# One decoder step on one core: the first projection chunk before the normalisation is known, its weights loaded ahead of the small vectors

## What is computed

```python
def _rmsnorm(x, g):
    y = xf * lax.rsqrt(jnp.mean(xf * xf, axis=-1, keepdims=True) + EPS)
    return (y * g.astype(jnp.float32)).astype(x.dtype)

# _mixer(h = _rmsnorm(x, norm_mix_g), ...)
proj = h @ w_in                                   # 1024 -> 7168 columns
cv, cg, q, f, v, og, ga, gb = jnp.split(proj, _split_offsets(), axis=-1)
u = cv * jax.nn.sigmoid(cg)
full = jnp.concatenate([conv_state.astype(u.dtype), u], axis=1)
c = lax.conv_general_dilated(full, conv_dw_w[:, None, :], ...)   # 31 taps, depthwise
...
# then the HGRN2 branch, gates, w_out, residual; norm; mixture of 32 experts; residual; norm
```

## Time and profile before

| | |
|---|---|
| median of three runs | 830.75 us (830.71 to 831.6) |
| the profiled execution | 830.96 us, its span 828.4 us |
| TensorE busy | 786.7 us, 95% of the span |
| TensorE weight loads | 453.0 us, 55% |
| VectorE busy | 246.6 us, 30% |
| ScalarE busy | 154.1 us, 19% |
| GpSimd busy | 120.8 us, 15% |
| moved by DMA | 267.99 MB, 324 GB/s over the span |

### The profile page before, as it was taken

How to read it: one execution, slowest core, us unless ns; L and a number is a source line. 1 busy time by engine, 2 the same in 40 slices (tenths; PEclk the granted TensorE clock), 3 DMA queues, 4 the chain that set the end, 5 groups by cost and what they waited for, 6 DMA issues and landing times.

```text
span 828.4 us, 9578 instructions
## 1 busy us (share of the span) xinstructions
PE 786.7 (95%) x3929; PEld 453.0 (55%) x3929; DVE 246.6 (30%) x528; ACT 154.1 (19%) x242; POOL 120.8 (15%) x139
## 2 busy tenths in 40 slices
PE   6999999999999999999999999999989988999996
PEld 4888888888788888873333333333323222333332
DVE  2159958586552222361001110111011011101102
ACT  3012422434302500140111111100100110010012
POOL 5100051656520000001110000002200000000001
PEclk9999999999999999999999999999999999999999
DMA  8824656768589682389999999999999999999992
GB/s 302 255 102 148 232 158 204 194 188 192 191 285 408 247 302 102 115 306 416 422 398 429 426 427 426 426 425 428 426 429 425 428 427 429 427 423 421 423 419 109
DMA packets 74388, 267.99 MB, mean 324 GB/s; under 512 B 5598, under 2 KB 37450, under 8 KB 58335
## 3 DMA queue, kind: packets, MB, share of 16 engines
q1 hardware_dynamic: 72666, 264.36, 81.9%
q0 software_dynamic: 528, 1.90, 0.6%
q10 hardware_dynamic: 1149, 1.09, 0.4%
HBM read 259.26 MB, written 8.55 MB: 323 GB/s over the span
## 4 chain that ended last, share of the span: by engine, by line
PE 78%; DMA 13%; POOL 3%; DVE 2%; issue 2%; ACT 1%; SPq 1%; DVEq 0%; POOLq 0%
PE bank L1889 22%; PE bank L1529 21%; PE bank L1927 11%; DMA slots<-in_w_expert_gate_dram 8%; PE bank L1785 7%; PE bank L1936 6%; DMA slot<-in_w_expert_gate_dram 4%; PE bank L1732 2%; PE bank L1572 2%; DMA slots<-in_w_in_dram 1%; PE bank L1916 1%; DVE early L1396 1%; ACT wrep L953 1%; PE bank L1853 1%; PE bank L1800 1%
## 5 line engine op out<-in xcount | busy, mean ns | idle before, releaser
L1529 PE MATMUL bank<-hT,slots 128*128 128x264 f32 x896 | 207.2, 391 | 0.2 <-DMA slots<-in_w_in_dram 0.2
L1889 PE MATMUL bank<-slots,hT 128*64 128x512 f32 x680 | 185.6, 595 | 7.7 <-DMA slots<-in_w_expert_gate_dram 7.7
L1529 PEld LDWEIGHTS bank<-hT,slots 128*128 128x128 f32 x896 | 170.0, 192 | 28.9 <-issue 0.6
L1396 DVE TENSOR_TENSOR early<-early,bank 128x512 f32<-128x512 f32 x16 | 11.0, 688 | 384.6 <-PE bank L1889 384.6
L1889 PEld LDWEIGHTS bank<-slots,hT 128*64 128x64 f32 x680 | 57.1, 137 | 109.0 <-issue 96.9
L1927 PE MATMUL bank<-slots,wrep 128*64 128x512 f32 x336 | 103.6, 596 | 5.4 <-ACT wrep L953 5.4
L1889 PE MATMUL bank<-slot,hT 128*64 128x512 f32 x256 | 73.7, 594 | 2.3 <-DMA slot<-in_w_expert_gate_dram 2.3
L767 POOL COPY hT<-early 128x512 f32 x30 | 17.6, 613 | 369.6 <-PE bank L1889 286.3
L1936 PE MATMUL bank<-hT,diag 128*128 128x512 f32 x128 | 59.2, 605 | 0.2 <-ACT hT L965 0.2
L1927 PEld LDWEIGHTS bank<-slots,wrep 128*64 128x64 f32 x336 | 32.1, 137 | 49.7 <-issue 41.0
L1098 DVE SCALAR_TENSOR_TENSOR slot<-slot,rows_buf 128x256 f32<-128x256 f32 x120 | 48.1, 478 | 0.0
(11 more groups left out here) (292 smaller groups left out, 756.7 us busy)
## 6 DMA issues: line engine op xcount, KB each, us to landing
slots<-in_w_expert_gate_dram SPq DMA_DIRECT2D x18, 2048.0 KB, 28.3
slots<-in_w_expert_down_dram SPq DMA_DIRECT2D x18, 2048.0 KB, 29.6
slots<-in_w_expert_up_dram SPq DMA_DIRECT2D x16, 2048.0 KB, 29.9
slots<-in_w_in_dram SPq DMA_DIRECT2D x14, 2048.0 KB, 9.6
slot<-in_w_expert_gate_dram SPq DMA_DIRECT2D x8, 2048.0 KB, 25.3
slots<-in_w_expert_up_dram SPq DMA_DIRECT2D x9, 1024.0 KB, 29.8
slots<-in_w_expert_gate_dram SPq DMA_DIRECT2D x8, 1024.0 KB, 22.8
slot<-in_w_expert_up_dram SPq DMA_DIRECT2D x4, 2048.0 KB, 29.2
```

Source lines behind the costliest of these rows:

```text
L1396: dve.tensor_tensor(act.rearrange("s (f c) -> s f c", f=FT), act.rearrange("s (f c) -> s f c", f=FT), bank[UP][:, :].rearrange("s (c f) -> ...
L1529: last = mm(out, w[:, a, t * P:(t + 1) * P], hT[:, a, :], start=(a == 0), stop=(a == KT - 1))
L1889: last = mm(out[sl, :], xe[:, a, sl], expert_view(p, kind, e, a // 4)[:, a % 4, :], start=(a == 0), stop=(a == KT - 1))
```

## The change

Nothing of what is computed is left out. In `xgain` x times the norm weight is kept, and chunk 0 is projected from that; its four tiles are multiplied by the root when DVE takes them from PSUM. `hT`, for all other chunks, is `xgain` times the root.

- The norm weight for the mixer is loaded first of all, alone (`gain_in`), and its transposition is the first of the `misc` ring. Chunk 0 is loaded behind x in two halves (channel tiles 0 to 3 and 4 to 7), each with a semaphore of its own. The other eight vectors and the taps are issued from ACT's queue, behind ACT's copies to `xT`.
- x is turned to four banks of their own (4, 5, 2, 3), first all eight tiles of tokens 0 to 127, then those of 128 to 255; the samples are turned before both to bank 7. PE also makes six matmuls whose results nobody reads (`keep_busy`).
- PE begins chunk 0 with tiles 0 and 1 side by side over channel tiles 0 to 3 (`first_tiles(0)`), spreads the root, then channel tiles 4 to 7, then tiles 2 and 3. The vectors and the taps are turned behind chunk 0, and the products for the convolution state are moved behind chunk 1.

```diff
+            sp.dma_start(vecr[0:KT, :], ins["norm_mix_g"][0].rearrange("(r c) -> r c", c=P)).then_inc(gain_in, 16)
             sp.dma_start(xtok[0:NB, 2, :], xs).then_inc(x_in[2], 16)
             for i in range(2):
                 sp.dma_start(xtok[:, i, :], xp[i * P:(i + 1) * P, :]).then_inc(x_in[i], 16)
...
-            for c in range(STREAM):
+            sp.dma_start(slot3(0)[:, 0:KT // 2, :], stream[0][0][:, 0:KT // 2, :]).then_inc(first_in, 16)
+            sp.dma_start(slot3(0)[:, KT // 2:, :], stream[0][0][:, KT // 2:, :]).then_inc(stream_in[0], 16)
+            for c in range(1, STREAM):
                 load(c)
...
+            se.wait_ge(x_gained, 1)
+            se.copy(xT[:, :, SEQ:T], xs_turned).then_inc(x_copied, 1)
+            for i in range(KT // 2):
+                se.wait_ge(x_gained, 2 * i + 3)
+                se.copy(xT[:, 2 * i:2 * i + 2, 0:SEQ], x_pair(i)).then_inc(x_copied, 1)
...
+                se.dma_start(vecr[row:row + r, :], flat).then_inc(vec_in, 16)
+                row += r
+            assert row == 76
+            se.dma_start(tapr, ins["conv_dw_w"][0]).then_inc(tap_in, 16)
...
+            for d in range(KT):
+                dve.wait_ge(x_turned, d // 2 + 2)
+                dve.tensor_scalar(xgain[:, d, 0:SEQ], x_pair(d // 2)[:, d % 2, :], vec[:, d:d + 1], None,
+                                  ALU.mult).then_inc(x_gained, 1)
             dve.wait_ge(rms_ready, 1)
...
+            def normed(d):
+                dve.wait_ge(x_gained, KT + 1)
+                dve.tensor_tensor(hT[:, d, :], xgain[:, d, :], rstd, ALU.mult).then_inc(hmix_ready, 1)
...
+            def first_values(c):
+                src = take(proj, ("cv", c))
+                dve.tensor_tensor(u[:, c, :], src[:, 0:T], rstd, ALU.mult).then_inc(P_dve, 1)
...
+            pe.wait_ge(*made("ones"))
+            keep_busy(2)
+            pe.wait_ge(gain_in, 16)
+            misc.before_write(pe, "gain")
+            tr(bank[misc.bank("gain")][:, 0:KT], vecr[0:KT, :], ident[0:KT, 0:KT]).then_inc(M_ready, 1)
+            pe.wait_ge(x_in[2], 16)
+            for d in range(KT):
+                last = tr(xs_turned[:, d, :], xtok[0:NB, 2, d * P:(d + 1) * P], ident[0:NB, 0:NB])
+            last.then_inc(x_turned, 1)
+            keep_busy(4)
+            pe.wait_ge(x_in[0], 16)
+            for d in range(KT):
+                turn_x(d, 0)
...
+            first_tiles(0)
+            spread_rstd()
+            first_tiles(1)
+            for t in range(2, 4):
+                in_tile(0, t)
+            pe.wait_ge(vec_in, 16 * 8)
+            misc.before_write(pe, "vec")
+            tr(bank[misc.bank("vec")][:, 0:76], vecr, ident[0:76, 0:76]).then_inc(M_ready, 1)
             pe.wait_ge(tap_in, 16)
...
-            for t in range(1, 4):
-                in_tile(0, t)
+            in_projection(1)
```

More of the change, by code:

```diff
@@ L431, in _ @@
                 sp.dma_start(xtok[:, i, :], xp[i * P:(i + 1) * P, :]).then_inc(x_in[i], 16)
[L433 to L442, removed]
             def load(c):
@@ L815, in _ @@
                 se.activation(xjunk[0:m, i, :], xtok[0:m, i, :], ACT.Square, accum_out=ss[0:m, i:i + 1]).then_inc(x_squared, 1)
[L816 to L820, removed]
+            se.wait_ge(x_gained, 1)
[3 more added lines that the diff above has]
+                se.copy(xT[:, 2 * i:2 * i + 2, 0:SEQ], x_pair(i)).then_inc(x_copied, 1)
+            row = KT
+            for name, lead in (("b_gates", 0), ("conv_dw_b", 0), ("conv_ln_g", 0), ("conv_ln_b", 0),
+                               ("hgrn_lb_param", None), ("hgrn_norm_g", 0), ("norm_ffn_g", 0), ("norm_final_g", None)):
+                a = ins[name] if lead is None else ins[name][0]
+                flat = a.rearrange("l (r c) -> (l r) c", c=P) if name == "hgrn_lb_param" else a.rearrange("(r c) -> r c", c=P)
+                r = flat.shape[0]
+                se.dma_start(vecr[row:row + r, :], flat).then_inc(vec_in, 16)
+                row += r
+            assert row == 76
+            se.dma_start(tapr, ins["conv_dw_w"][0]).then_inc(tap_in, 16)
+            se.wait_ge(*made("eps"))
             se.wait_ge(lb_diff, 2)
@@ L1489, in turn_groups, with keep_busy @@
                     last.then_inc(ring.ready, 1)
+            def keep_busy(n):
+                for _ in range(n):
+                    mm(bank[0][:, 0:P], ones[:, 0:P], ident[:, :], start=True, stop=True)
             def turn_x(d, i):
-                t0, m = TOK_TILES[i]
-                return tr(bank[misc.bank(("x", d))][:, t0:t0 + m], xtok[0:m, i, d * P:(d + 1) * P], ident[0:m, 0:m])
-            pe.wait_ge(c_ident, 1)
-            for i in (2, 0):
-                pe.wait_ge(x_in[i], 16)
-                for d in range(2):
-                    turn_x(d, i)
@@ new lines, in _, with spread_rstd @@
+            for d in range(KT):
+                turn_x(d, 0)
+            pe.wait_ge(x_in[1], 16)
+            for d in range(KT):
+                last = turn_x(d, 1)
+                if d % 2:
+                    last.then_inc(x_turned, 1)
+            def spread_rstd():
+                pe.wait_ge(diag_ready, 3)
+                pe.wait_ge(x_copied, 1)
+                misc.before_write(pe, "rsb")
+                for i, (t0, m) in enumerate(TOK_TILES):
+                    last = mm(bank[misc.bank("rsb")][:, t0:t0 + m], ones[0:m, 0:P], diag[0:m, i, 0:m], start=True, stop=True)
@@ L1619, in turn_rows, with first_tiles @@
                 last.then_inc(M_ready, 1)
-            in_tile(0, 0)
+            def first_tiles(half):
+                pe.wait_ge(*((stream_in[0], 16) if half else (first_in, 16)))
+                for a in range(4 * half, 4 * half + 4):
+                    pe.wait_ge(x_gained, a + 2)
+                    for t in range(2):
+                        last = mm(bank[proj.bank(("cv", t))][:, 0:T], slot3(0)[:, a, t * P:(t + 1) * P], xgain[:, a, :],
+                                  start=(a == 0), stop=(a == KT - 1))
+                        if a == KT - 1:
+                            last.then_inc(P_ready, 1)
+            first_tiles(0)
[6 more added lines that the diff above has]
+            tr(bank[misc.bank("vec")][:, 0:76], vecr, ident[0:76, 0:76]).then_inc(M_ready, 1)
             pe.wait_ge(tap_in, 16)
```

95 lines of the change are left out of this document (47 added, 48 removed).

## The result

The changed kernel takes 822.01 us (median of four runs, 820.96 to 823.95), the kernel before 830.73 in the runs beside them: a ratio of 0.9888, 95% interval 0.9873 to 0.9903. Two later series of the changed kernel beside the kernel before gave 0.9893 and 0.9877. It is 8.7 us faster; the forecast was 5.2, and its range ended at 822.9.

A forecast was written before the change was run, and what follows sets the result against it. PE was taken as the limit behind the first projection matmul, loads in the experts: 6.2 us earlier, less 0.9 and 0.1, saves 5.2, so 825.6 us (chance 0.51; own range 824.2 to 826.8, full range 822.9 to 828.2).

The forecast's parts named there:

- That the start carries over: From the first projection matmul to the experts' stage: the earlier start is carried over in full; rival that it is not, chance 0.06.
- The start of chunk 0: PE begins chunk 0 at 10.0 us (bounds 9.3 and 12.3) instead of 16.16, which is 6.2 us earlier.
- the price of 0.28: Turning x ahead of chunk 0: a 128-column record costs about 0.28 us at the lower clock level, pauses included.
- the old load's excess of 5.0 us: Chunk 0's load before the change: 10.53 us for 5.5 us of data; the taps' 31 rows estimated at 2.6 us.
- with the 2.2 us of the lower clock level taken as unchanged: First 16 records of chunk 0: TensorE's lower clock level still costs 2.2 us, so nothing is saved there.
- the rivals with 0.20: At chunk 0's start: the clock is already up, giving 2.2 us more, 823.4 us; chance 0.20.
- I count nothing: PE's 1.8 us wait for POOL: DVE's 1.7 us lead on `u` could shorten only this; counted nothing, bound 1.8.
- The late vectors: Vectors and taps needed behind chunk 0: taken as hidden; rivals 2.1 us wait, 827.7, chance 0.07; 10.6 us, 836.2, chance 0.04.
- the prediction's estimate by turns between the queues: Taps' load on ACT's queue: with packet-by-packet turns, 31 rows take at most twice 2.6 us, landing at about 24.
- the forecast's 11 us of cover: Vectors and taps: last issued at about 16.5 us, wanted by PE at 27.6, so a landing may take 11 us.
- The products behind chunk 1: Convolution-state products moved behind chunk 1: cost what they cost before (1.68 us), and let DVE begin `u` 1.7 us earlier.
- The spread of the root and DVE's part: Around chunk 0: the root's spread adds 0.9 us to PE's path; DVE's multiplications and diagonal lie beside PE's work.

## Why the prediction was wrong

**That the start carries over** was right. PE behind chunk 0 was busy without a break, the experts' loads run at the same rate, and what was won at 57 us is there at the end.

**The start of chunk 0** was right in mechanism and nearly in size: 10.0 was said, 9.5 measured, with the load at 9.5 (said: 9.7) and x turned at 9.4 (said: 9.5 to 11). Sixteen transpositions in one go take 3.4 us, 0.21 each; the price of 0.28 was too high, and 0.23 still was. The 12 records in 3.35 us behind it are eight large transpositions and four small ones mixed, not pauses: the run with small ones mixed in has the same 0.82 us for three without any wait. That two things were late at once is what the run with the taps behind chunk 0 shows. Of the old load's excess of 5.0 us the taps were 2.6. That 31 rows go through one engine is what the Trainium skill has (page "DMA: Bandwidth & Descriptors", section "Why a DMA increments its semaphore by 16 and not by 1"), and the traces agree: 31 packets one after another, and 2.6 us estimated against 2.1 (ahead of the half) and 2.6 (ahead of the whole chunk) measured.

No run puts the root back ahead of chunk 0 and leaves the rest, so what the deferred root is worth by itself is not shown. An estimate from the traces: POOL has the root at 9.5 us in the changed kernel, and the diagonal (1.05 before), its spread (0.9), the copy of `rstd` (0.43) and the first tile of `hT` (0.42) would put chunk 0 at 12.3 us, 2.8 later than now.

**The step that failed is "with the 2.2 us of the lower clock level taken as unchanged".** 2.0 us came with the clock. It stood among the rivals with 0.20, and the argument against it was that 3.4 us of turning x had not raised the level before. But those rows were of turning large and small pieces mixed, and the changed kernel turns sixteen large ones without a break, behind eight records of filler. The order of TensorE's instructions ahead of the prediction showed just that, and it was not weighed. The clock alone would have left the time inside the range, at 823.6; with the terms below it fell out.

**"I count nothing" for the wait for POOL** was too low by 0.8 to 1.4 us against the three profiles of the changed kernel, and the mechanism for the bound, DVE's lead, was wrong: the wait follows the landing of `v_rows`. How much of it is the change's is not shown.

**The microsecond outside the span** was in no step. The profiled execution's 2.56 us were carried along as a constant.

Together: 5.2 + 0.5 (start) + 2.0 (clock) + 0.8 to 1.4 (POOL) − 0.3 (taps) + 0.9 (outside) is 9.1 to 9.7, where the three series have 8.7, 9.2 and 9.9. That two of the pieces the range counted as alternatives came at once, with one that it did not know, is why 822.9 was too high for its end.

**The late vectors** cost 0.3 us. The taps took 10.6 us from ACT's issue to landing, not the 7.5 of the prediction's estimate by turns between the queues (from 16.5 to about 24), so this was close: the forecast's 11 us of cover were just used up. The turns were not the error: the 31 packets took 5.8 us, near the twice 2.6 of the estimate. The first of them came 3.8 us after the issue, and for that no term stood in it.

**The products behind chunk 1** were called a move at no cost. They are, but leaving them would have cost everything. The prediction never asked when their operand is there: POOL's product ended at 32.9 before, PE came at 33.25, and nearly every microsecond won ahead of it would have been a wait.

**The spread of the root and DVE's part** were right (0.76 and hidden).

## What to carry to other kernels

When the start of a busy engine is moved earlier, list every operand that it meets behind the start, with the time at which it is there: what was just in time before is late now, and one of them can take back all that was won. The pieces of such a change don't add up: putting back one of them cost 4.1 us (the taps), 4.6 (the whole chunk), 4.4 (the mixed turning) or 10 (the products), and all together had won 8.7. Stands of 2.3 to 6.1 us ahead of dense matmuls were paid almost twice here, once as a wait and once at the lower clock level; stands of up to 1.6 us were paid once. A load of 31 rows ahead of one that is waited for is not small. Price a sequence of large transpositions from large ones in a row, not from rows in which small ones are mixed.

## What the runs showed of the hardware

- In this kernel TensorE's level came up before chunk 0 only when x was turned in one unbroken sequence of full-size transpositions (first clock record at 7.2 to 9.5 us in ten profiles of eleven, at 15.0 to 20.5 in the six with small ones mixed in); with small ones mixed in, eleven unused matmuls in the pauses didn't bring it up. With the unbroken sequence alone, and no matmul ahead of it, it was up in one of two profiles. What the chip wants of the engine is not shown by that.
- A 128x128 float32 transposition follows the one before it in 0.213 us at the lower level and in 0.11 at the upper; with a small one behind every second, three take 0.82 us at the lower level.
- The granted clock in the profile's rows reads 1.00 up to the first change that it records, also where the durations say half (9 records in 4.12 us).
- 62 KB in 31 rows went as 31 packets one after another. They cost the load behind them 2.1 and 2.6 us, and took 10.6 us themselves from a second queue while the first was loaded, 3.8 of it before the first packet.
- The same work can have one microsecond more or less outside the span, by one matmul in PE's program (median 2.7 us without it, 1.74 with it).
